# Stick-breaking attention of a two-block decoder: scores turned to queries on partitions, suffix sums by a scan

## The reference

```
A[t,s] = sigmoid(z_ts) * prod_{s<j<t} (1 - sigmoid(z_tj)),  s < t

for blk in range(S // SB_BLOCK):                 # 2 blocks of 128 queries
    z = einsum('bhtd,bhsd->bhts', qb, kb) * dh ** -0.5
    strict = s_idx < t_idx
    log_1m = where(strict, log_sigmoid(-z), 0.0)
    suffix = cumsum(log_1m, axis=3, reverse=True) - log_1m
    a = where(strict, exp(log_sigmoid(z) + suffix), 0.0)
    outs.append(einsum('bhts,bhsd->bhtd', a, vb))
```

## Time and profile before

| what | value |
|---|---|
| median of 3 runs | 1694.37 us (1694.32 to 1694.82) |
| profiled execution, its own time | 1695.04 us |
| span from first to last instruction | 1693.3 us |
| TensorE matmul busy | 1647.2 us (97%) |
| VectorE busy | 1164.3 us (69%) |
| ScalarE busy | 948.0 us (56%) |
| GpSimd busy | 372.8 us (22%) |
| TensorE's share of the chain that ended last | 77% |
| granted TensorE clock, mean | 0.996 |
| stick-breaking stage, first block to last `sbo` block | about 1267 to 1404 us from the start |

### The profile page before, as it was taken

How to read it: one execution, slowest core, us unless ns; L and a number is a source line. 1 busy time by engine, 2 the same in 40 slices (tenths; PEclk the granted TensorE clock), 3 DMA queues, 4 the chain that set the end, 5 groups by cost and what they waited for, 6 DMA issues and landing times.

```text
span 1693.3 us, 32581 instructions
## 1 busy us (share of the span) xinstructions
PE 1647.2 (97%) x13128; PEld 1589.6 (94%) x13128; DVE 1164.3 (69%) x1966; ACT 948.0 (56%) x1717; POOL 372.8 (22%) x335
## 2 busy tenths in 40 slices
PE   7999999999998999999999999999999999999997
PEld 6998989999997889999999999999999998999996
DVE  7999887555577865556676756766686756576666
ACT  6677765544455666444666545544465655454443
POOL 0100011244352222445411202001242121100025
PEclk9999999999999999999999999999999999999999
DMA  5433334555542246666535535566564444445653
GB/s 202 137 121 106 124 109 137 166 174 179 173 134 80 79 156 187 188 185 188 174 125 163 175 102 173 176 183 179 174 186 125 129 151 132 132 133 172 182 182 110
DMA packets 76326, 257.54 MB, mean 152 GB/s; under 512 B 8464, under 2 KB 12560, under 8 KB 75920
## 3 DMA queue, kind: packets, MB, share of 16 engines
q1 hardware_dynamic: 76176, 255.45, 48.9%
HBM read 254.37 MB, written 1.05 MB: 151 GB/s over the span
## 4 chain that ended last, share of the span: by engine, by line
PE 77%; DVE 10%; ACT 6%; issue 4%; POOL 2%; DMA 0%; POOLq 0%; DVEq 0%; SPq 0%; ACTq 0%
PE pb L143 76%; DVE WL L162 3%; DVE TMP L174 2%; ACT SCR L152 2%; DVE SCR L174 2%; POOL X L162 1%; ACT WH L152 1%; ACT L159 1%; PE pb L146 1%; DVE SCR L162 1%; POOL SQ L162 1%; ACT ASH L152 1%; ACT TMP L152 0%; DVE HNL L174 0%; ACT SCR L153 0%
## 5 line engine op out<-in xcount | busy, mean ns | idle before, releaser
L162 DVE TENSOR_TENSOR WL<-RAW,WH 128x1024 fp32r<-128x1024 f32 (+4 forms) x514 | 608.1, 1185 | 14.7 <-ACT WH L152 14.5
L143 PE MATMUL pb<-HNH,WH 128*128 128x256 f32 (+1 forms) x2056 | 594.8, 289 | 6.3 <-issue 2.4
L152 ACT ACTIVATE WH<-RAW 128x1024 fp32r<-128x1024 f32 (+4 forms) x514 | 507.1, 989 | 147.8 <-PE pb L143 145.6
L143 PE MATMUL pb<-HNH,WL 128*128 128x256 f32 (+1 forms) x2056 | 583.0, 284 | 0.0
L143 PE MATMUL pb<-HNL,WH 128*128 128x256 f32 (+1 forms) x2056 | 582.8, 283 | 0.0
L143 PE MATMUL pb<-ASH,WH 128*128 128x256 f32 (+1 forms) x1560 | 449.2, 288 | 7.2 <-DVE WL L162 3.9
L143 PE MATMUL pb<-ASH,WL 128*128 128x256 f32 (+1 forms) x1560 | 443.4, 284 | 0.0
L143 PE MATMUL pb<-ASL,WH 128*128 128x256 f32 (+1 forms) x1560 | 442.7, 284 | 0.0
L143 PEld LDWEIGHTS pb<-HNH,WH 128*128 128x128 f32 x2056 | 387.9, 189 | 14.1 <-issue 4.0
L143 PEld LDWEIGHTS pb<-HNH,WL 128*128 128x128 f32 x2056 | 388.3, 189 | 0.0
L143 PEld LDWEIGHTS pb<-HNL,WH 128*128 128x128 f32 x2056 | 386.7, 188 | 1.2
(11 more groups left out here) (158 smaller groups left out, 1725.9 us busy)
## 6 DMA issues: line engine op xcount, KB each, us to landing
RAW<-in_w_gu SPq DMA_DIRECT2D x88, 512.0 KB, 3.8
RAW<-in_w_up SPq DMA_DIRECT2D x64, 512.0 KB, 3.5
RAW<-in_w_down SPq DMA_DIRECT2D x64, 512.0 KB, 3.5
RAW<-in_w_ssd SPq DMA_DIRECT2D x48, 512.0 KB, 3.5
RAW<-in_w_xkv SPq DMA_DIRECT2D x32, 512.0 KB, 3.8
RAW<-in_w_mlin SPq DMA_DIRECT2D x24, 512.0 KB, 3.6
RAW<-in_w_fd SPq DMA_DIRECT2D x32, 384.0 KB, 3.0
RAW<-in_w_sbqkv SPq DMA_DIRECT2D x24, 512.0 KB, 3.8
```

The source lines that it names most:

```text
L143: return self.eng.matmul(o, l, r, start=start, stop=stop, skip_group_check=skip) if self.eng else Nothing()
L152: return self.eng.activation(o, i, f, bias=bias, scale=scale)
L162: return self.eng.tensor_tensor(o, a, b, op) if self.eng else Nothing()
```

## The change

Scores are taken with queries on partitions, so that a suffix sum runs along the columns: VectorE does it by one backward `tensor_tensor_scan` of 384 elements per head, with a factor of 0 where a tile of another query block begins or where the diagonal is passed (`again`). The sum is subtracted from z, ScalarE takes the exponential, GpSimd multiplies the two diagonal tiles with a mask (`past`, 256 columns). TensorE then turns the weights by three transposes per head into banks 5 and 7, ScalarE copies them to WT, and the output matmuls are as before. The values of two groups are taken as one pair of blocks with tokens on partitions (`pe_v_rows`), evicted by ScalarE with the root turned to rows (RT2, two transposes at slot 2). The columns of `sbqkv` are put in the order q, k, q, k, v, v for each two groups. The pieces of a group lie at slots 3c+3 to 3c+9, k = 0 to 6, where TensorE has work at k = 0, 4 and 5. The first three blocks of `sbo` are begun at slots 28 to 30 with 7 of their 8 chunks. The memory parts are spread over every third slot. The constants shrink by 512 columns.

```diff
@@ evicted
-            act = name in ("up0", "up1", "wk", "xkv0", "xkv1") or name == "mlin" and m % 6 in (2, 3)
+            act = name in ("up0", "up1", "wk", "xkv0", "xkv1") or name == "mlin" and m % 6 in (2, 3) or (
+                name == "sbqkv" and m % 6 in (4, 5))
@@ sb_cores
-            return [(c, n - 3 * c - 3) for c in range(8) if n - 3 * c - 3 in (0, 2, 3)]
+            return [(c, n - 3 * c - 3) for c in range(8) if 0 <= n - 3 * c - 3 <= 6]
@@ pe_sb_core
-                for i in range(2):
-                    t = q.transpose(banks[5][:, 128 * i:128 * i + 128], vT3[:, s, 128 * i:128 * i + 128], cc("ident"))
...
-                    q.matmul(z[:, 0:256], key[:, 0:128], qry, True, False, True)
-                    q.matmul(z[:, 256:384], key[:, 128:256], qry[:, 128:256], False, False, True).then_inc(*zq(c, e))
-            elif k == 2:
-                for e in range(2):
-                    z, L = banks[3 + e], Ls[:, s, e, :]
-                    q.wait_ge(*lm[c, e])
-                    q.matmul(z[:, 0:256], cc("ntge"), L[:, 0:256], False, False, True)
-                    q.matmul(z[:, 256:384], cc("ntge"), L[:, 256:384], False, True, True)
-                    q.matmul(z[:, 128:256], cc("nones"), L[:, 256:384], False, True, True).then_inc(*zs(c, e))
+                    q.matmul(z[:, 0:256], qry[:, 128:256], key, True, False, True)
+                    q.matmul(z[:, 256:384], qry[:, 0:128], key[:, 0:128], False, True, True).then_inc(*zq(c, e))
+            elif k == 4:
+                for e in range(2):
+                    b, w = banks[TURNED[e]], Ws[:, s, e, :]
+                    q.wait_ge(*wm[c, e])
...
+                    q.transpose(b[:, 0:128], w[:, 256:384], cc("ident"))
+                    q.transpose(b[:, 128:256], w[:, 0:128], cc("ident"))
+                    q.transpose(b[:, 256:384], w[:, 128:256], cc("ident")).then_inc(*wt(c, e))
@@ pe_sb
-            for n in range(24, 28):
-                if n in (24, 26):
-                    pe_fill(q, "v", 1, n // 2 - 11)
+            for n in range(24, 31):
+                if n < 28:
+                    j = n % 2
+                    if j == 0:
+                        ids = v_blocks(q, 1, n // 2 - 11)
+                    pe_v_rows(q, ids, mem_parts(1, "v", n // 2 - 11), j)
+                else:
+                    i = q.block("sbo", 0, n - 28)
+                    pe_bank_free(q, i)
+                    q.wait_ge(*lo[i])
+                    pe_chunks(q, i, T2, ax, 0, 7)
+                    begun.append(i)
@@ act_sb_core
+            if k < 2:
+                e = k
+                L, z = Ls[:, s, e, :], banks[3 + e][:, 0:384]
+                q.wait_ge(*zq[c, e])
...
+            elif k < 4:
+                e = k - 2
+                w = Ws[:, s, e, :]
+                q.wait_ge(*zd[c, e])
+                q.activation(w, w, ACT.Exp).then_inc(*wex(c, e))
+            elif k == 4:
+                for e in range(2):
+                    q.wait_ge(*wt[c, e])
+                    if c > 1:
+                        q.wait_ge(*sbo[c - 2, e])
+                    q.activation(WT[:, s, e, :], banks[TURNED[e]][:, 0:384], ACT.Copy).then_inc(*wcp(c, e))
@@ act_sb
+                if n % 3 == 2:
+                    act_mem(q, "mem1", n // 3)
+                if n % 6 == 5:
+                    q.wait_ge(*rtd["sb"])
+                    q.wait_ge(*use[i])
+                    for t in range(2):
+                        q.activation(VT[:, n // 6, t, :], bank_of(i - 1 + t)[:, 0:256], ACT.Copy,
+                                     RT2[:, t:t + 1]).then_inc(*eva(i - 1 + t))
@@ dve_sb_core
+            if k in (1, 2):
+                e = k - 1
+                L, z = Ls[:, s, e, :], banks[3 + e][:, 0:384]
+                q.wait_ge(*ll[c, e])
+                q.stt(L, z, 0.0, L, ALU.max, ALU.add).then_inc(*lsp(c, e))
+                q.wait_ge(*lsp[c, e])
+                q.scan(L[:, ::-1], cc("again"), L[:, ::-1], 0.0, ALU.mult, ALU.add).then_inc(*cum(c, e))
+                q.wait_ge(*cum[c, e])
...
+                q.tt(Ws[:, s, e, :], z, L, ALU.subtract).then_inc(*zd(c, e))
@@ pool_sb
-                            q.tt(L, L, cc("s384"), ALU.mult).then_inc(*lm(c, e))
+            for c in range(8):
+                for e in range(2):
+                    w = Ws[:, c % 2, e, 128:384].rearrange("p (a k) -> p a k", k=128)
+                    q.wait_ge(*wex[c, e])
+                    q.tt(w, w, bc(cc("past"), 2), ALU.mult).then_inc(*wm(c, e))
```

More of the change, by code:

```diff
@@ L32 @@
 NCOL = _at
[L33 removed]
+NFIRST = COLS["m384"][0]
 KC = {
@@ L2703, in pe_sb_core @@
                 for e in range(2):
                     o = banks[6][64 * e:64 * e + 64, :]
[L2705 to L2708, removed]
+                    v = 128 * (c % 2) + 64 * e
+                    w = WT[:, s, e, :]
+                    q.wait_ge(*wcp[c, e])
@@ L2709, in pe_sb_core @@
+                    q.matmul(o[:, 0:256], VT[:, c // 2, 0, v:v + 64], w[:, 0:256], True, False, True)
+                    q.matmul(o[:, 128:256], VT[:, c // 2, 1, v:v + 64], w[:, 256:384], False, True,
                              True).then_inc(*sbo(c, e))
         def pe_sb(q):
-            xs = hn_chunks("sb")
+            xs, ax = hn_chunks("sb"), as_chunks("sb", 0, 8, T2)
             for n in range(24):
-                pe_block(q, "sbqkv", 0, n, T2, xs)
+                j = n % 6
+                if j > 3:
+                    i = AT["sbqkv", 0, n - j + 4]
+                    q.block("sbqkv", 0, n)
+                    pe_v_rows(q, (i, i + 1), xs, j - 4)
+                else:
+                    pe_block(q, "sbqkv", 0, n, T2, xs)
@@ L2722, in pe_sb @@
                 for c, k in sb_cores(n):
                     pe_sb_core(q, c, k)
-            pe_post(q, "sbo", as_chunks("sb", 0, 8, T2), rms["sb"])
-            pe_post_norm(q, "sbo", rms["sb"])
+            pe_post(q, "sbo", ax, wcp[7, 1], begun, 7)
+            pe_post_norm(q, "sbo", wcp[7, 1])
         def act_sb_core(q, c, k):
             s = c % 2
-            if k == 0:
+            if k < 2:
[3 more added lines that the diff above has]
+                if c > 1:
+                    q.wait_ge(*zd[c - 2, e])
+                q.activation(L, z, ACT.Abs).then_inc(*la(c, e))
+                q.wait_ge(*la[c, e])
+                q.activation(L, L, ACT.Exp, -1.0).then_inc(*lx_(c, e))
+                q.wait_ge(*lx_[c, e])
+                q.activation(L, L, ACT.Ln, 1.0, cc("one")).then_inc(*ll(c, e))
+            elif k < 4:
[4 more added lines that the diff above has]
+            elif k == 4:
@@ L2769, in dve_sb_core @@
             s = c % 2
-            if k == 0:
-                q.wait_ge(*vtt[c])
-                if c > 1:
[L2773 to L2785, removed]
+            if k in (1, 2):
[6 more added lines that the diff above has]
+                q.wait_ge(*cum[c, e])
+                if c > 1:
+                    q.wait_ge(*wt[c - 2, e])
+                q.tt(Ws[:, s, e, :], z, L, ALU.subtract).then_inc(*zd(c, e))
+            elif k == 6:
                 dve_part(q, "sb", c, ASL[:, c, 0:T2], banks[6][:, 0:T2], ASH[:, c, 0:T2])
@@ L3013 @@
     put("tri", le)
-    put("ntge", -(j[:, None] >= j[None, :]).astype(np.float32))
-    put("nones", -np.ones((128, 128), np.float32))
     put("ones", np.ones((128, 128), np.float32))
@@ L3018 @@
     put("m384", np.concatenate([le, one, le], 1))
-    put("s384", np.concatenate([lt, one, lt], 1))
-    neg = np.where(lt > 0, 0.0, -1e30).astype(np.float32)
-    put("n384", np.concatenate([neg, 0 * one, neg], 1))
+    again = one - np.eye(128, k=-1, dtype=np.float32)
+    turn = one.copy()
+    turn[0, 127] = 0.0
+    put("again", np.concatenate([turn, again, again], 1)[:, ::-1])
+    put("past", lt.T)
     put("cmask", np.where(j[None, :] <= j[:, None], 0.0, -1e30).astype(np.float32))
```

146 lines of the change are left out of this document (79 added, 67 removed), and 1 row of the table _at.

## The result

The changed kernel takes 1684.62 us (median of 4 runs, 1683.99 to 1685.36) against 1694.44 us: ratio on record 0.9933, 95% interval 0.9921 to 0.9945 (the quotient of the two medians, 0.9942, lies inside it). Applied to the 1694.37 us of before, 0.9933 gives 1683.0 us, so the gain is 9.8 us by the medians and 11.4 by the ratio, against 8.9 forecast. The sign was right, and so was the engine that sets the pace; the price of the transposes was not. The range began at 1683.5, just above the time by the ratio. The profiled execution took 1685.00 us (span 1683.2), 10.04 less than that of before.

What follows compares the result with a forecast made beforehand. TensorE was taken to bound the groups. Savings of 8.1 us in eight groups plus 1.3 for the old wait, less 0.5 for the root's turn, gave 8.9: 1694.37 to 1685.5 us, range 1683.5 to 1690.5.

Steps and rivals of the forecast that it cites:

- The bound: In the groups TensorE, busy 12.50 of 12.50 us, sets the pace; helpers have 4.7 and 5.1 us of room.
- Transposes: Six transposes of weights per group on TensorE, priced at 0.92 us, bounds 0.80 to 1.75.
- the root's turn: Two transposes between blocks at slot 2, done once, costing TensorE 0.5 us.
- The group: TensorE's non-block work per group falls from 3.98 to 2.97 us: 1.01 saved, 8.1 over eight; period 11.49.
- The old wait: TensorE's 1.34 us loss before the last output, to subtraction and exponential, is hidden by begun `sbo` blocks.
- The end of the new stage: Slots 28 to 30 and after: new waits of TensorE cost 0 us, 0.5 at most.
- The weight of `sbo` block 4: Next item late at the stage's end: ready 3.5 us after block 0, against TensorE work equal to within 0.1.
- VectorE and ScalarE: Per group VectorE is busy 9.40 us and ScalarE 8.7 or 9.5, of 11.49; no wait reaches TensorE.
- The estimate from the half throughput: VectorE's scan of 384 elements at twice a 0.56 us instruction: 1.12 us, VectorE 9.6 per group.
- Rival 1: Helpers stall TensorE in part: each group loses 0.3 us and the end 1.5, 1689 us; chance 20%.
- Rival 2: VectorE becomes the bound through slow backward scans: 12 to 25 us lost, 1697 to 1710 us; chance 6%.
- rival 3: Transposes cost 1.75 us and new waits in slots 24 to 30 replace the old one: 1693 us; chance 7%.

Runs made afterwards that it cites:

- experiment 2: Changed kernel with each group's six transposes issued twice: median 1691.11 us against 1684.65; stage 133.05 us, 5.27 longer.
- experiment 3: Changed kernel with a second, unread VectorE scan of 384 elements per head: median 1684.82 us; stage 128.29 us, 0.5 more.
- experiment 5: Changed kernel with ScalarE's copy of the turned weights issued twice: stage 128.59 us, 0.8 more; period 11.22 us.
- experiment 1: Kernel before, with the cross attention's division of weights left out and a two-column copy instead: its four transposes cost 0.44 us, not 0.71.
- experiment 6: Changed kernel with ScalarE evicting the memory's first value pair before the last group's head 1 logs: stage 126.51 us, 1.3 less; median 1684.48 against 1684.65.
- experiment 7: Kernel before, with two `sbo` blocks begun around the last group's output: stage 136.48 us, 1.25 less; median 1695.22 against 1695.13. Spreading memory values first gave 138.34.
- experiment 4: Changed kernel with the scan running forward instead of backward, which changes the sums: stage 127.82 us, no difference in scan time.

## Why the prediction was right or wrong

**The bound: right.** TensorE sets the pace before and after; each 0.66 us put on it costs 0.66, while 1.9 us more on VectorE or 0.8 on ScalarE leave the period as it is (experiments 2, 3, 5; VectorE's 1.9 cost 0.5 once, at the second group).

**Transposes: the step that failed.** I priced six at 0.92 from the piece in the next stage, with 0.22 of entry. That entry was a wait for VectorE, and without it the row itself was 0.05 shorter (experiment 1); 0.92 less these 0.27 is the 0.65 that was measured. Over eight groups that is 2.2 us of gain left out, and with the root's turn (0.22, not 0.5) 2.5. I had named 0.80 as the lower bound and 0.09 as the least entry; both were too high, and so was the range's lower end: with 0.65 and the root's 0.22 in it the sum is 11.4 us, a time of 1683.0 us.

**The group: otherwise right.** Scores and output pieces kept their price. 3.98 fell to 2.69 (the measured 11.21 less 8.52) and not 2.97; eight groups give 10.3 us, not 8.1.

**The old wait: right.** 1.34 forecast, 1.25 measured by itself, in the kernel before (experiment 7).

**The end of the new stage: a term missed.** I took 0 to 0.5 us. TensorE lost 1.25 us, from 1363.25, where the next matmul was due, to 1364.50, at slot 26, where I had not followed the bank of the memory's values to its eviction behind the last group's logs (experiment 6). The weight of `sbo` block 4, which I had named as late next, was not: the last 21.33 us of the stage are one piece of the chain.

**The sum.** Groups 10.3, old wait 1.25, root's turn 0.2 and new wait 1.25: 10.3 + 1.25 - 0.2 - 1.25 = 10.1, measured 9.95; some 0.15 us are not assigned. That my 8.9 is within 1.1 of this is in part luck: the two errors, +2.5 and -1.25, go against each other. By the stage alone the time would be 1684.4 us, inside the range; the 1683.0 by the ratio is outside, and the 1.4 us between them are not explained.

**VectorE and ScalarE: right.** 9.4 forecast, 8.7 to 9.6 measured; ScalarE 8.7 to 9.5 against 8.5 to 9.3. The scan was 0.96 against 1.02. The estimate from the half throughput in the Trainium skill (DVE: opcode table, instruction layouts, handler registers and perf-mode slots; Datapath and trigger behaviour) was 1.12; the row of 0.68 was the better guide.

**Rivals.** Rival 1 (helpers stall TensorE in part) happened at one place and for another reason than contention: the order of ScalarE's queue at slot 26. VectorE and GpSimd do hold each other up (experiment 3, and the split of 1.75 us above), but in the changed kernel where no wait of TensorE hangs on it. Rival 2 is excluded by experiments 3 and 4. Of rival 3 the price is excluded by the measured 0.65; its new wait came, at 1.25 us.

## What to carry to other kernels

When a price is taken from a neighbouring stage, look first whether the instruction's operand was ready: a gap that ends with the record of the engine that makes the operand may be a wait, even if the list of waits does not name it, and a wait does not come along. Experiment 1 is the test. In a kernel bound by one in-order engine, moving work to helpers is worth its full length on that engine as long as their lateness stays inside the banks' room; here a helper busy for 98% of the period left the period as it was, with little room to spare. After such a change follow each bank to its eviction in the irregular slots at the end, where an eviction behind a long piece of another group is the next wait.

## What was unexpected of the hardware

- Transposes of 128 x 128 float32 between blocks cost nothing to enter: six took 0.65 us with 0.08 to leave, and six more 0.66, so 0.11 each. A float32 matmul piece over 64 rows or columns paid 0.09 to enter.
- A scan costs the same in both directions: 0.96 us for 384 elements on 128 partitions; 256 on 4 partitions took 0.68.
- VectorE could be kept busy for 10.99 of 11.20 us without the period moving; the stage was 0.5 us longer.
- A VectorE scan or weight split and a GpSimd mask hold each other up: a mask of 0.74 us took 1.35, a scan of 0.96 took 1.32, a split of 1.22 took 1.75.
- The mean granted clock of whole runs lay between 0.991 and 0.997, and the lower values went with the longer times (1699.30 us at 0.992, 1693.18 at 0.997, the same kernel); the stage, at granted clock 1.00 in its windows, repeated within 0.1 us.
